# Layer 0's MLP in parts of 10, 10 and 12 blocks, the first two with Strassen quads; the modulation's ring cut to two tiles; ScalarE's closing of blocks moved by one unit

## What is computed

```python
mod = c_act @ ada_w[i] + ada_b[i]                 # 2 layers x 6144 numbers, K = 1024
sh1, sc1, gt1, sh2, sc2, gt2 = jnp.split(mod, 6, axis=-1)
...
h = _modulate(_rmsnorm(x, norm_g[i, 1]), sh2, sc2)
x = x + gt2[:, None, :] * (jnp.square(jax.nn.relu(h @ mlp_w1[i])) @ mlp_w2[i])   # 1024 -> 4096 -> 1024
```

## Time and profile before

| what | value |
|---|---|
| median of 3 runs | 2530.1 us (2527.66 to 2536.54) |
| the profiled execution, its own time | 2526.72 us |
| its span | 2524.9 us |
| mean granted clock of TensorE | 0.992 |
| TensorE busy (matmuls) | 2459.2 us, 97% |
| VectorE busy | 1520.8 us, 60% |
| ScalarE busy | 1002.6 us, 40% |
| GpSimd busy | 233.3 us, 9% |
| the chain that ended last | 86% TensorE, 6% VectorE, 3% ScalarE |

### The profile page before, as it was taken

One profiled execution on the slowest core, in us unless ns is written; L12 is line 12 of the kernel. 1 busy time (PEld: TensorE's weight loads), 2 busy tenths in 40 slices (PEclk: granted clock), 3 DMA queues, 4 the chain that ended last, 5 costly groups with the idle time before them and its releaser, 6 DMA issues.

```text
span 2524.9 us, 42032 instructions
## 1 busy us (share of the span) xinstructions
PE 2459.2 (97%) x17974; PEld 2066.9 (82%) x17974; DVE 1520.8 (60%) x2375; ACT 1002.6 (40%) x1539; POOL 233.3 (9%) x216
## 2 busy tenths in 40 slices
PE   8999999999999999999999999999999999999998
PEld 7888888876777887798988889888668987889887
DVE  7865756647845446675755666575355744557444
ACT  4224313337643233545434333343256434333322
POOL 0110100000220000000000110111221000111110
PEclk9999999999999999999999999999999999999999
DMA  8663666622210003364542346245212422335422
GB/s 336 199 193 125 195 190 192 192 90 84 84 43 4 5 29 105 107 153 129 152 118 82 100 109 175 92 121 155 67 42 78 140 80 65 107 105 147 123 74 86
DMA packets 92410, 294.84 MB, mean 117 GB/s; under 512 B 10320, under 2 KB 12624, under 8 KB 91712
## 3 DMA queue, kind: packets, MB, share of 16 engines
q1 hardware_dynamic: 74608, 232.39, 29.0%
q0 software_dynamic: 17616, 59.76, 9.3%
HBM read 287.92 MB, written 4.19 MB: 116 GB/s over the span
## 4 chain that ended last, share of the span: by engine, by line
PE 86%; DVE 6%; ACT 3%; issue 2%; DMA 1%; SPq 1%; POOL 0%; DVEq 0%; ACTq 0%
PE ps L726 21%; PE ps L732 18%; PE ps L730 18%; PE ps L742 3%; PE ps L745 3%; PE ps L771 3%; PE ps L776 3%; PE ps L774 3%; DVE WLs L1986 1%; PE ps L783 1%; ACT WHs L1361 1%; PE ps L924 1%; PE ps L937 1%; DMA raw<-in_f1d_a 1%; SPq L2937 1%
## 5 line engine op out<-in xcount | busy, mean ns | idle before, releaser
L1986 DVE TENSOR_TENSOR WLs<-raw,WHs 128x1024 fp32r<-128x1024 f32 (+3 forms) x454 | 485.2, 1069 | 287.0 <-ACT WHs L1361 284.6
L726 PE MATMUL ps<-HH,WHs 128*128 128x512 f32 x1728 | 651.8, 400 | 5.7 <-ACT HH L1432 2.2
L1361 ACT ACTIVATE WHs<-raw 128x1024 fp32r<-128x1024 f32 (+3 forms) x472 | 438.1, 931 | 454.1 <-PE ps L732 244.7
L732 PE MATMUL ps<-HH,WLs 128*128 128x512 f32 x1434 | 559.4, 390 | 2.9 <-DVE WLs L1986 2.9
L730 PE MATMUL ps<-HL,WHs 128*128 128x512 f32 x1434 | 558.5, 389 | 0.0
L726 PEld LDWEIGHTS ps<-HH,WHs 128*128 128x128 f32 x1728 | 324.8, 189 | 78.7 <-issue 12.1
L732 PEld LDWEIGHTS ps<-HH,WLs 128*128 128x128 f32 x1434 | 269.1, 188 | 61.4 <-DVE WLs L1986 4.6
L730 PEld LDWEIGHTS ps<-HL,WHs 128*128 128x128 f32 x1434 | 269.5, 188 | 55.0 <-issue 2.2
L771 PE MATMUL ps<-HT,WHs 128*128 128x256 f32 x812 | 227.8, 281 | 6.8 <-DVE X L2065 3.4
L774 PE MATMUL ps<-HT,WHs 128*128 128x256 f32 x812 | 226.9, 279 | 0.4 <-DVE HT L2246 0.2
L776 PE MATMUL ps<-HT,WLs 128*128 128x256 f32 x812 | 226.8, 279 | 0.2 <-DVE WLs L1986 0.2
(11 more groups left out here) (463 smaller groups left out, 3791.3 us busy)
## 6 DMA issues: line engine op xcount, KB each, us to landing
ada<-in_adaw POOLq DMA_DIRECT2D x80, 512.0 KB, 4.7
raw<-in_mw_0b SPq DMA_DIRECT2D x32, 512.0 KB, 3.6
raw<-in_f1gu_b SPq DMA_DIRECT2D x20, 512.0 KB, 3.6
raw<-in_f2gu_b SPq DMA_DIRECT2D x20, 512.0 KB, 3.5
raw<-in_f1gu_a_m SPq DMA_DIRECT2D x18, 512.0 KB, 3.5
raw<-in_w_in_m SPq DMA_DIRECT2D x18, 512.0 KB, 3.4
raw<-in_f2gu_a_m SPq DMA_DIRECT2D x18, 512.0 KB, 3.5
ada<-in_adaw SPq DMA_DIRECT2D x16, 512.0 KB, 16.6
```

The lines of the kernel that those rows point to most:

```text
L726: pe.matmul(o[m], WHs[:, s, w], hi, start=k == 0, stop=False)
L732: t = pe.matmul(o[m], WLs[:, s, w], hi, start=False, stop=k == DEPTH_K[name] - 1)
L1361: act.activation(WHs[:, SLOT[v], 0:n], piece(v), ACT.Copy).then_inc(*S.up("w_hi", ("hi", v)))
L1986: dve.tensor_tensor(WLs[:, s, 0:n], piece(v), WHs[:, s, 0:n].bitcast(F32), SUB).then_inc(*S.up("w_lo", ("lo", v)))
```

## The change

PROJ gives layer 0's MLP three parts of 10, 10 and 12 blocks. Parts a and b use quads five chunks deep; part c is as before, with 12 chunks. `mw1_0a` is now of kind "g" (4 blocks chunk by chunk, not 8). Tiles HT0, wsum0 and T0 hold what HT, wsum and T2 hold elsewhere. To make room the ring of the modulation gets two tiles instead of six. In projections of quads VectorE makes a dot only at product 3 of each quad. GpSimd's adding DMAs for the new quads stand between its loads of the modulation, at places given by a table. ScalarE closes blocks of quads one product later than before, and loads its table for the square root at product 3 of the first quad. The negated gate is made per layer.

```diff
-NADA = 6
+NADA = 2
...
-        ("mw1_0a", "e", 16, 8), ("mw2_0a", "m", 8, 16), ("mw1_0b", "m", 16, 8), ("mw2_0b", "m", 8, 16),
+        ("mw1_0a", "g", 10, 8), ("mw2_0a", "s", 8, 10), ("mw1_0b", "m", 10, 8), ("mw2_0b", "s", 8, 10),
+        ("mw1_0c", "m", 12, 8), ("mw2_0c", "m", 8, 12),
...
-MLP = ["ab", "abc"]
+MLP = ["abc", "abc"]
...
+        HT0 = at_("HT0", WK + 32832, [128, 2, 5, 1792], F32R)
+        wsum0 = at_("wsum0", WK + 104512, [128, 640])
+        T0 = at_("T0", WK + 107072, [128, 2, 512])
...
-        ada = at_("ada", WK + 98304, [128, NADA, 1024])
+        ada = at_("ada", WK + 111168, [128, NADA, 1024])
...
             def residual(name):
+                waiting = []
+
                 def evac(m):
                     _, to, tag = RESIDUAL[name]
                     if not tag:
                         return
-                    for n, m in closed(m):
-                        if n == 0:
+                    ready = closed(m)
+                    if isinstance(m, tuple):
+                        ready, waiting[:] = waiting[:], ready
+                        if m == (0, 3):
                             warm(ACT.Sqrt)
+                        if m == (BLOCKS[name] // 2 - 1, 6):
+                            ready += waiting
+                    elif m == 0:
+                        warm(ACT.Sqrt)
+                    for n, m in ready:
                         on.wait_ge(*S.at("X", to, m))
                         square(tag, n, X[:, m])
...
                     if KIND[two] == "s":
                         dense(one, hidden_fast(one), within if part == "a" else after)
-                        dense(two, last_lows(one)(residual(two)), after)
+                        if part == "a":
+                            on.wait_ge(*S.at("mod", 6 * layer + 5))
+                            dve.tensor_scalar(ngate[:, 8 * layer:8 * layer + 8], mod[:, 48 * layer + 40:48 * layer + 48], -1.0, None,
+                                              MUL).then_inc(*S.up("v_mod", ("ngate", layer)))
+                        dense(two, last_lows(one)(residual(two)), (lambda i: after(i) if i % 7 == 3 else None) if after else None)
...
+            beside = {48: ("mw2_0a", 0), 53: ("mw2_0a", 1), 54: ("mw2_0a", 2), 55: ("mw2_0a", 3),
+                      62: ("mw2_0b", 0), 67: ("mw2_0b", 1), 68: ("mw2_0b", 2), 69: ("mw2_0b", 3)}
             for u in range(16, 96):
+                if u in beside:
+                    added(beside[u][0], [beside[u][1]])
                 on.wait_ge(*(S.at("dot", u - NADA) if u >= 16 + NADA else S.at("ada", 7)))
                 pool.dma_start(ada[:, u % NADA], D["adaw"][u]).then_inc(*S.up("ada_in%d" % (u % NADA), ("ada", u), by=16))
```

More of the change, by code:

```diff
@@ L450 @@
 MEMORY = memory_order()
-RESIDUAL = {"cw_out": ("x0", "c", "m0"), "mw2_0a": ("c", "c2", None), "mw2_0b": ("c2", "r", "r"),
+RESIDUAL = {"cw_out": ("x0", "c", "m0"), "mw2_0a": ("c", "c2", None), "mw2_0b": ("c2", "c3", None), "mw2_0c": ("c3", "r", "r"),
             "w_o": ("back", "m", "m1"), "mw2_1a": ("m", "m2", None), "mw2_1b": ("m2", "m3", None), "mw2_1c": ("m3", "fg", "fg"),
@@ L456 @@
             "f2d_a": ("f2", "f2b", None), "f2d_b": ("f2b", "end", "end")}
-GATE = {"cw_out": (0, 2), "mw2_0a": (0, 5), "mw2_0b": (0, 5), "w_o": (1, 2), "mw2_1a": (1, 5), "mw2_1b": (1, 5), "mw2_1c": (1, 5),
+GATE = {"cw_out": (0, 2), "mw2_0a": (0, 5), "mw2_0b": (0, 5), "mw2_0c": (0, 5), "w_o": (1, 2), "mw2_1a": (1, 5), "mw2_1b": (1, 5), "mw2_1c": (1, 5),
         "f1d_a": 0.5, "f1d_b": 0.5, "w_out": 1.0, "wo": 1.0, "f2d_a": 0.5, "f2d_b": 0.5}
@@ L638, in minus_gate, with inputs, staged @@
         def minus_gate(name, m):
-            return ngate[:, m:m + 1] if isinstance(GATE[name], tuple) else -GATE[name]
+            if not isinstance(GATE[name], tuple):
+                return -GATE[name]
+            n = 8 * GATE[name][0] + m
+            return ngate[:, n:n + 1]
+        def inputs(src):
+            return HT0 if src[0:5] == "mw1_0" else HT
+        def staged(src):
+            return T0 if src[0:5] == "mw1_0" else T2
         def piece(v):
@@ L643, in piece, with loaded @@
             if WANT[v][1] != "s":
[L644 removed]
+                return loaded(v, RAW[v], n)
             i = WANT[v][3]
             return wsum2[:, 0:n] if i == 2 else quarter(v, [0, 1, None, 4, 2, 3, 4][i])
[L648 to L649 removed]
+        def loaded(v, r, n):
+            if PLACE[r] == NRAW:
+                return (wsum0 if v < HALT else wsum)[:, 0:n]
+            return raw_[:, PLACE[r], 0:n]
         def quarter(v, q):
[L652 removed]
+            return loaded(v, RAW[v - WANT[v][3], q], 128 * WANT[v][4])
         def gains(name):
@@ L756, in fast @@
                 src = name.replace("mw2", "mw1")
+                HT = inputs(src)
                 for a in range(BLOCKS[name] // 2):
@@ L805, in pe_program @@
                 norm("m0")
[L806 to L809, removed]
+                for part in "ab":
+                    dense("mw1_0" + part, h, lambda k: ("HL", "m0", k))
+                    fast("mw2_0" + part)
+                dense("mw1_0c", h, lambda k: ("HL", "m0", k))
+                dense("mw2_0c", hm, lambda k: ("mlo", "mw1_0c", k))
             norm("r")
@@ L2857, in pool_program, with added @@
                 pool.dma_start(o[:, :], D[i]).then_inc(*S.up("table_in", ("tables",), by=16))
+            def added(name, pairs):
+                for a in pairs:
+                    v = FIRST[name] + 7 * a
+                    for i, q, part in ((1, 1, 0), (4, 2, 2)):
+                        on.wait_ge(*S.at("raw", v, q))
+                        pool.dma_start(quarter(v, q), D[name][a, part], accum_op=ADD).then_inc(*S.up("w_added%d" % q, ("sum", v + i), by=16))
+            beside = {48: ("mw2_0a", 0), 53: ("mw2_0a", 1), 54: ("mw2_0a", 2), 55: ("mw2_0a", 3),
+                      62: ("mw2_0b", 0), 67: ("mw2_0b", 1), 68: ("mw2_0b", 2), 69: ("mw2_0b", 3)}
             for u in range(16, 96):
+                if u in beside:
+                    added(beside[u][0], [beside[u][1]])
                 on.wait_ge(*(S.at("dot", u - NADA) if u >= 16 + NADA else S.at("ada", 7)))
@@ L2879, in pool_program @@
                         pool.tensor_tensor(A[:, f], A[:, f], H8[:, f], MUL).then_inc(*S.up("g_mix", ("a2", f)))
-            def added(name, pairs):
-                for a in pairs:
-                    v = FIRST[name] + 7 * a
-                    for i, q, part in ((1, 1, 0), (4, 2, 2)):
-                        on.wait_ge(*S.at("raw", v, q))
-                        pool.dma_start(quarter(v, q), D[name][a, part], accum_op=ADD).then_inc(*S.up("w_added%d" % q, ("sum", v + i), by=16))
             def ffn(n):
```

27 lines of the change are left out of this document (15 added, 12 removed).

## The result

The changed kernel takes 2558.11 us (median of 4 runs, 2554.05 to 2562.34) where the kernel before, on the same chip, takes 2529.27 us. The ratio is 1.0111, 95% interval 1.0095 to 1.0127: it is 1.1% slower. The sign was forecast, the size was not: 2539.1 was predicted and 2551.0 was the upper end. The profiled execution took 2558.55 us, its span 2556.8.

What follows compares the result with a forecast made beforehand. TensorE was taken as the bound, its matmuls filling 97% of the span. Terms -9.9 - 5.3 + 1.1 + 4.9 + 17.7 (GpSimd's queue) + 0.5 gave +9.0 us on 2530.1, so 2539.1 us, range 2522 to 2551.

Steps and rivals of the forecast that it cites:

- columns: Layer 0's MLP: fewer matmul columns on TensorE, 256-column matmuls at 0.1177 us each, gain 9.9 us if nothing waits.
- mw1_0a: Projection mw1_0a as kind "g": waits, with a dot on VectorE delaying the late low part, loss 1.1 us.
- first quads: Start of mw2_0a and mw2_0b: 2.4 us of waits each, as in f1d_b's beginning, loss 4.9 us.
- transitions: Layer 0's MLP: other dots and loads lie hidden under matmuls; 0.5 us loss allowed for transitions.
- gate of the dot: Quads 1 to 3 of both parts: waiting for the previous quad's dot makes a 13.6 us loop against 12.36, 1.25 each.
- the load ahead in the queue: GpSimd's queue, quads 1 to 3 of both parts: the modulation load ahead delays the adding DMA, 1.7 us per quad.
- ScalarE's order: f1d_b: making the high parts before closing blocks removes three 1.42 us stalls and one of 0.97, gain 5.3 us.
- x: Extra landing time of an adding DMA from the modulation load ahead in GpSimd's queue: 1.7 us, bounds 0 to 3.6.
- The rival with x about 3.5: Pair behind the load as slow as the trace's slow pair: 28.5 us, sum +19.8, 2550 us; chance 0.14.
- The half clock: Layer 0's MLP: TensorE's granted clock read as 1.00, the upper level; no term for a lower clock.
- the rival that it brings nothing: f1d_b: VectorE is the bound, so ScalarE's new order gains 0; sum +14.3, 2544 us; chance 0.08.
- The rival that the quarters come in time: Quads of mw2_0a and mw2_0b: added quarters land before TensorE waits, queue term 0, sum -8.7, 2521.4 us; chance 0.17.

Runs made afterwards that it cites:

- e1: Changed kernel with GpSimd's adding DMAs for quads 1 to 3 of both parts one modulation load earlier in its queue: 2523.36 us, ratio 0.9991.
- e3: Changed kernel with each pair of adding DMAs behind the wait for the same dot, but issued ahead of the modulation load: 2529.14 us, ratio 1.0011.
- e2: Kernel before with only ScalarE's later closing of blocks added: 2520.04 us, ratio 0.9978.
- e7: Changed kernel with adding DMAs moved earlier and the quads' eight dots moved to mw1_0c's first eight pieces: 2515.45 us, ratio 0.9960 to the kernel before.
- e6: Changed kernel with 256 of 1024 columns in the six modulation loads directly ahead of the late pairs: 2542.45 us, ratio 1.0066.
- e5: Changed kernel with ten idle products on TensorE between products 0 and 1 of quads 1 to 3 of both parts: 2541.46 us, ratio 1.0062.
- e8: Changed kernel with five idle products in those quads and the six loads cut to 256 of 1024 columns: 2540.12 us, ratio 1.0046.
- e4: Kernel before with only the modulation's ring cut from six tiles to two: 2529.02 us, ratio 1.0009.
- a2: Changed kernel measured again, with no further edit: 2552.35 us, ratio 1.0098 to the kernel before.

## Why the prediction was right in sign and wrong in size

The ledger of layer 0's MLP and f1d_b; measured figures come from the profiles of the runs named.

| step | predicted | measured | from |
|---|---|---|---|
| columns, mw1_0a, first quads, transitions | -3.4 | +1.2 | e1's MLP end |
| gate of the dot, 6 x 1.25 | +7.5 | +3.4 | e3 less e1 |
| the load ahead in the queue, 6 x 1.7 | +10.2 | +27.7 | changed less e3 |
| ScalarE's order | -5.3 | -5.6 | e2's ratio |
| sum | +9.0 | +26.7 | |

The two medians of the changed kernel against those of before in their batches give +28.8 and +26.8; the ledger closes to about 2 us. That the three steps of the MLP add up to its 32.3 us is by their making; the test is the last line against the medians.

*Columns, right in price.* Matmuls of 256 columns stood 0.12 us apart in every quad at full clock, and the plain blocks took their columns. The estimate from the Trainium skill, "TensorE: Matmul & The Clock Gate", section "Back-to-back issue gap", a loss of 19 us, is not borne out: e7's parts take 51.6 and 51.0 us for 420 such matmuls each.

*mw1_0a, right.* 56.2 us for 54.4 of columns, 0.8 more than the 0.96 that was over before; +1.1 was forecast.

*First quads, under-sized.* I took f1d_b's quads as the model and its 2.4 us per part for small waits. f1d_b has no dots. With one per quad mw2_0a and mw2_0b took 10.1 us over their columns in e1; without them it was 3.8, near the 4.9 of the sum. I had priced the dots of mw1_0a and called the others hidden without counting VectorE's work inside a quad.

*The gate, over-sized.* 1.25 us was the loop of 13.6 less 12.36, a quad without any wait. e1's quads took 13.4 and 13.8 us each (53.7/4, 55.2/4), so the gate could add only what was left: from the first draw of one quad to that of the next e3 took 13.1 to 14.4 us, 13.8 in the mean, so the loop itself was reckoned well and its price was taken against a quad that the program does not reach. That this error and the last nearly cancel is luck.

*The load ahead, the first of the two steps that failed.* "I take **1.7**, near the queue's own arithmetic": the mechanism, its place, its six quads and the order of events were as written, but x was 2.2 to 3.7, mean 2.8, six times 1.1 us more. My arithmetic for the low value, in which the adding DMA lands some 2 us after the load ahead of it, was refuted by e6: the load of 128 KB is down 2.4 us after its issue, so by that arithmetic it would not have held up the adding DMA at all, and the landing was still at 6.1 to 7.2 us. The rival with x about 3.5 was the nearer one.

*The half clock, the second step that failed: a term put at nothing without a reason.* The prediction read a clock of 1.00 off and kept it, and none of its rows shows what a stall of 3 us does to it. The trace of before did hold such a row. Behind layer 0's MLP TensorE waits 3.59 us, and for most of the 4 us that follow its clock is at the lower level (matmul, then a window of 3 us):

```profile
564.32 1.65 PE L726 MATMUL ps<-M0H,WHs 128*128 128x512 f32 x4 [3.59 <-ACT M0H L1555]
...
565.00:568.00 3.00, 3.00 (x9) 0.50 0.00 0
```

So the cost could have been seen coming. The change made stalls of 3 to 4 us, and each brought 3.4 or 6.8 us at half speed, in the links of the very loop that sets the quad: at least 8.2 us by e5. In this loop a slower product 1 puts off the next dot, and so the next pair, one for one. Landings and clock together, 6 x 2.8 + 8.2 = 25.0, are nearly all of the 27.7, though the two overlap a little, as e8 shows (11.8 us for both edits, 14.3 for their sum). For the forecast's x = 2.8 alone the sum would have been 9.0 + 6.6 = 15.6 and the time 2545.7, inside the range; the clock took it out. The Trainium skill, "TensorE: Matmul & The Clock Gate", section "Part 1: The HAM clock gate (the "warmup" mystery)", calls the lower clock the default, which sustained activity releases. The trace agrees with it in kind (0.50 at each of the six stalls).

*ScalarE's order, right.* -5.3 forecast, -5.6 (95%: -8.3 to -3.0) measured alone and f1d_b 4.5 us shorter in e2's profile; the rival that it brings nothing falls.

*The ring of two* was priced at nothing by itself: +1.2 us in e4's MLP end, not told from none by the times.

*The rival that the quarters come in time* falls with the rows at 299.15: VectorE stood 4.82 us for the DMA. The stalls stood 17.7 to 18.8 us apart, outside even the 14.5 to 16 that the prediction named as its mark; that alone would have told that the size was off.

What stays open: why a short load ahead costs most of what a long one costs, and whether the add is held by the load's end or by a cost per DMA. The base of 4.5 us is not firm either: the other adding DMA of each quad of f1d_b, onto raw, took 5.5, 6.6, 6.4 and 7.3 us in the trace of before, with nothing of GpSimd's ahead of it. It is also open what the last 2 to 4 us of small waits in e7's quads are made of.

## What to carry to other kernels

When a transfer on the critical path is put into a queue, ask what is issued directly ahead of it: moving a pair of DMAs by one place in the program (e1) was worth 31 us here, and swapping load and pair behind the same wait (e3) 28. Price a new stall with its sequel, not only with its length: look whether the work behind it runs at half clock, as it did here behind 2.8 us and more, and whether that work is a link of the loop that makes the next stall. And a gain in columns is only there if the other engines can keep up inside the shortened stage: count their work per quad, side jobs too, before calling them hidden.

## What the runs showed of the hardware

- TensorE's granted clock fell from 1.00 to 0.50 at each of the six stalls in the first profile of the changed kernel. At the three of 2.8 to 3.0 us it fell 0.7 to 1.3 us after work had resumed and was low for 3.4 us; at the three of 3.6 to 4.1 us it fell 0.6 to 1.0 us before work resumed and was low for 6.8 us. With 2.4 us of idle products in the gap and 1.2 to 1.4 us left idle, the clock over part a was 1.00; in part b a gap with 2.09 us left idle brought one more dip. A dip can come without a long stall too: in e3 it was 0.68 over four microseconds in the first quad (row below), where three waits of 0.61, 0.37 and 0.62 us end within 2 us, and 1.00 in the later quads of part a.

```profile
266.00:270.00 4.00, 3.01 (x13) 0.68 0.49 166
```

- At the same place of the quad, an adding DMA of 320 KB landed 4.2 to 4.8 us after issue with nothing of GpSimd's directly ahead of it (e3), 6.6 to 8.4 behind a load of 512 KB issued 0.54 us earlier (the changed kernel twice, e5), and 5.9 to 7.5 behind one of 128 KB (e6, e8). Elsewhere the first of these is no constant: adding DMAs that stood alone in the queue took 4.4 to 7.3 us in f1d_b of before and 4.9 to 7.0 in e7. The second of two adding DMAs landed after 7.9 us with nothing but the first ahead of it (e3), and after 9.1 behind load and first (a2).
- The stage from da1 to layer 1's norm, which no edit aims at, scattered by 11 us over ten profiles (403.3 to 414.2), where the end of layer 0's MLP repeated within 1.3 us in two profiles of the changed kernel: stage lengths of a single profile are not equally firm.
